# Seven products instead of eight in the up projection of a feed-forward

## Chip, cores, metric

One core of a Trainium2 chip. The metric is device time in microseconds (us), 3024.73 as the median of three runs.

## What is computed

One inference step of a one-layer encoder over 2048 prompt tokens and 128 sample tokens, 17 token tiles of 128, width 1024. After the attention and pooling mixers, the mix gives x1, and then:

```python
def conv_ffn(h, conv_hist, w_up, w_dw, b_dw, w_down):
    up = h @ w_up                       # 1024 -> 2 x 2816
    ext = concat([conv_hist, up])
    c = ext[:, 0:T] * w_dw[0] + ext[:, 1:T + 1] * w_dw[1] + ext[:, 2:T + 2] * w_dw[2] + b_dw
    a, b = split(c, 2)
    return (silu(a) * b) @ w_down, ext[:, -2:]
x1 = layer_norm(ALPHA * x + mix)
x2 = layer_norm(ALPHA * x1 + ffn + sigmoid(x1 @ w_pg) * (p @ w_pe))
```

Everything is float32. Each matrix operand is held as a high part (rounded, fp32r) and a low part (the rest), and a product is three matmuls: high x high, low x high, high x low.

## The kernel before, in words

Six phases run one after the other: project, heads and sample attention, attend, mix, ffn. The change touches the last two.

**mix** (line 1857) goes over the 17 token tiles. PE multiplies the mixed heads by w_o, ACT, DVE and POOL norm the result to x1, PE turns it (128 x 128 transposes, `turn`), ACT copies the turned tile to `x1_t` and splits it, PE multiplies it by w_pg (`gates`), ACT takes the sigmoid into `gate`, DVE forms ALPHA * x1 + gate * embedding there, and SP stores `x1_t` and `gate`. At its end the first weights and token pieces of the ffn are loaded and split (`AHEAD`).

**ffn** (line 2293) takes the tokens in three blocks of 6, 6 and 5 tiles (`BLOCKS`; the last holds the sample tokens). For a block it goes over 22 feature tiles f, two to a pair. An f has two halves, s = 0 (a, goes through silu) and 1 (b). The up projection of an f (`rows` and `part` of PE) is, for each half and each half of the block's tokens, 8 slices of the contraction x 3 matmuls: 2 x 2 x 24 = 96 matmuls, of 384 tokens (384 and 256 in the last block), into four PSUM banks. ACT copies a bank to `up` and begins the convolution (tap 2 and bias) into `cv`; DVE adds taps 1 and 0 (`convolve`); ACT takes silu; DVE multiplies the halves (`gate`) into `h`; ACT makes its high part and POOL its low part (`product_hi`, `product_lo`). After each pair PE multiplies by two tiles of w_down (`downs`: 12 matmuls of 512 columns a token tile), and DVE adds the results to `y` in SBUF (`add`). After the last pair of a block `y` is normed (`normalise`, `centre`).

Weights come in units of 128 x 1024 (512 KB), six to a pair, through three raw buffers: SP loads, ACT makes the high part (L2540), POOL the low part (L2467). The high and low parts of the six have places of their own (`EVEN`, `DOWN`, `ODD`). The order on each engine is written out by hand; each engine works through its own queue in order and waits on semaphores. PE's order in a loop step is `rows(2q + 2)`, `downs(q)`, `rows(2q + 3)`.

## Time and profile before

| | us |
|---|---|
| runs | 3021.55, 3024.73, 3024.91 |
| span of the profiled execution | 3021.1 |
| feed-forward, from about | 1442 |
| PE busy | 2938.2 |

An instruction's row has its line, engine, operation, tiles (buffer numbers left out), shape, and durations; `[x <- engine tile line]` is idle time before it and what ended it. Matmuls overlap in the rows, so the pace is read from starts. DVE is VectorE, ACT ScalarE, POOL GpSimd, SP the queue that issues DMAs, PEld the weight loads. The profile has one execution's own span; no other time of that execution is given.

### The profile page before, as it was taken

To read this page: it belongs to the slowest core of one execution; us is meant where nothing else is said; L and a number is where in the kernel's file an instruction comes from. 1 tells how busy PE (TensorE), PEld (TensorE's weight loads), DVE (VectorE), ACT (ScalarE), POOL (GpSimd) and SP (SyncE) were. 2 spreads that over 40 slices of the span, in tenths; PEclk is the share of its full clock that TensorE was granted. 3 is DMA by queue.
4 is the path that set the end of the run, shared out by engine and by line. 5 is a ranking of instruction groups with operands and counts; after the bars stand their busy time and mean duration, and the time that the engine had idled before them with its cause. 6 is when DMAs were issued, how large, how long until landed. Compare 5 with 4: busy or idle time off the path is not lost.

```text
span 3021.1 us, 43561 instructions
## 1 busy us (share of the span) xinstructions
PE 2938.2 (97%) x15389; PEld 2586.1 (86%) x15389; DVE 1618.7 (54%) x2178; ACT 1352.3 (45%) x2632; POOL 1393.3 (46%) x830
## 2 busy tenths in 40 slices
PE   8998999999999899999999999999999999999997
PEld 6877787777776688887999999999999998999996
DVE  5635776787776544443434444464444447454446
ACT  4342555877787222222433333443434344444443
POOL 5342554666766422222434343474343447443445
PEclk9997898999999999999999999999999999999998
DMA  4227452122213322222412121242121224221221
GB/s 137 87 66 144 137 174 58 43 55 52 47 43 130 120 89 89 89 89 96 175 53 72 56 69 56 96 155 70 56 69 56 69 70 150 102 72 67 80 72 61
DMA packets 161774, 262.10 MB, mean 87 GB/s; under 512 B 48352, under 2 KB 91072, under 8 KB 160288
## 3 DMA queue, kind: packets, MB, share of 16 engines
q1 hardware_dynamic: 161664, 260.69, 27.7%
q8 instruction: 62, 1.02, 0.1%
q14 instruction: 48, 0.39, 0.0%
HBM read 204.76 MB, written 55.88 MB: 86 GB/s over the span
## 4 chain that ended last, share of the span: by engine, by line
PE 51%; DVE 1%; POOL 0%; issue 0%; DVEq 0%; ACTq 0%
PE ff_u L84 12%; PE ff_u L86 12%; PE ff_u L85 11%; PE ff_d L84 6%; PE ff_d L85 6%; PE ff_d L86 6%; DVE ff_y L2682 0%; DVE ff_y L2731 0%; DVE ff_stats L2714 0%; POOL ff_y L2517 0%; POOL ff_rstd L2507 0%; DVEq L2297 0%; DVE ff_mv L2716 0%; DVE ff_neg_mean L2718 0%; POOL ff_offset L2509 0%
## 5 line engine op out<-in xcount | busy, mean ns | idle before, releaser
L2467 POOL TENSOR_TENSOR ff_w_lo<-ho_raw,ff_w_hi 128x1024 fp32r<-128x1024 f32 x99 | 242.9, 2467 | 491.1 <-ACT ff_w_hi L2540 491.1
L2467 POOL TENSOR_TENSOR mx_w_lo<-ho_raw,mx_w_hi 128x1024 fp32r<-128x1024 f32 x97 | 276.0, 2859 | 230.9 <-ACT mx_w_hi L2540 230.9
L2661 DVE SCALAR_TENSOR_TENSOR ff_cv_a<-ff_up_a,ff_taps,ff_cv_a 128x768 f32<-128x768 f32 (+1 forms) x132 | 154.7, 1172 | 346.9 <-ACT ff_cv_a L2589 338.9
L2682 DVE TENSOR_TENSOR ff_y<-ff_y,ff_d 128x512 f32<-128x512 f32 x374 | 239.6, 681 | 146.3 <-PE ff_d L86 146.2
L2661 DVE SCALAR_TENSOR_TENSOR ff_cv_b<-ff_up_b,ff_taps,ff_cv_b 128x768 f32<-128x768 f32 (+1 forms) x132 | 122.7, 929 | 305.4 <-ACT ff_cv_b L2589 296.8
L1564 POOL TENSOR_TENSOR at_p_lo<-at_p,at_p_hi 128x512 fp32r<-128x512 f32 (+2 forms) x160 | 187.6, 1173 | 163.9 <-ACT at_p_hi L1601 162.2
L84 PE MATMUL ff_u<-ho_hi,mx_w_hi 128*128 128x384 f32 (+1 forms) x690 | 224.9, 326 | 0.7 <-ACTq L2533 0.7
L86 PE MATMUL ff_u<-ho_lo,mx_w_hi 128*128 128x384 f32 (+1 forms) x690 | 225.0, 326 | 0.0
L85 PE MATMUL ff_u<-ho_hi,mx_w_lo 128*128 128x384 f32 (+1 forms) x690 | 224.8, 326 | 0.0
L1594 ACT ACTIVATE at_p<-at_s 128x512 f32<-128x512 f32 (+1 forms) x320 | 170.2, 532 | 111.1 <-PE at_s L1790 56.0
L1706 DVE TENSOR_TENSOR at_p_lo<-at_p,at_p_hi 128x512 fp32r<-128x512 f32 (+1 forms) x160 | 187.3, 1171 | 45.5 <-ACT at_p_hi L1601 44.6
L84 PE MATMUL ff_u<-ho_hi,ff_w_hi 128*128 128x384 f32 x630 | 205.1, 326 | 0.0
L86 PE MATMUL ff_u<-ho_lo,ff_w_hi 128*128 128x384 f32 x630 | 205.0, 325 | 0.0
L85 PE MATMUL ff_u<-ho_hi,ff_w_lo 128*128 128x384 f32 x630 | 205.0, 325 | 0.0
L1601 ACT ACTIVATE at_p_hi<-at_p 128x512 fp32r<-128x512 f32 (+1 forms) x320 | 179.0, 560 | 0.0
L2580 ACT ACTIVATE ff_up_b<-ff_u 128x384 f32<-128x384 f32 x110 | 54.2, 493 | 268.8 <-PE ff_u L86 268.8
L84 PE MATMUL ff_d<-ff_w_hi,ff_h_hi 128*128 128x512 f32 x408 | 159.1, 390 | 4.4 <-DVE ff_y L2682 4.4
L2473 POOL TENSOR_TENSOR ff_h_lo<-ff_h,ff_h_hi 128x768 fp32r<-128x768 f32 (+1 forms) x66 | 118.2, 1791 | 91.3 <-ACT ff_h_hi L2600 91.3
L2674 DVE TENSOR_TENSOR ff_h<-ff_cv_a,ff_cv_b 128x768 f32<-128x768 f32 (+1 forms) x66 | 158.0, 2393 | 3.6 <-ACT ff_cv_a L2611 0.4
L85 PE MATMUL ff_d<-ff_w_hi,ff_h_lo 128*128 128x512 f32 x408 | 159.1, 390 | 0.0
L86 PE MATMUL ff_d<-ff_w_lo,ff_h_hi 128*128 128x512 f32 x408 | 159.1, 390 | 0.0
L2540 ACT ACTIVATE ff_w_hi<-ho_raw 128x1024 fp32r<-128x1024 f32 x99 | 103.3, 1049 | 123.2 <-DMA ho_raw<-in_w_ffn_p 123.2
(496 smaller groups left out, 8863.7 us busy)
## 6 DMA issues: line engine op xcount, KB each, us to landing
ho_raw<-in_w_ffn_p SPq DMA_DIRECT2D x196, 512.0 KB, 3.6
ho_raw<-in_x SPq DMA_DIRECT2D x17, 512.0 KB, 4.3
mx_m_raw<-scratch_mix_t SPq DMA_DIRECT2D x17, 512.0 KB, 5.2
scratch_x_t<-mx_work SPq DMA_DIRECT2D x17, 512.0 KB, 3.2
scratch_y<-mx_work SPq DMA_DIRECT2D x17, 512.0 KB, 3.0
ff_y<-scratch_y SPq DMA_DIRECT2D x17, 512.0 KB, 6.2
out_y<-ff_y SPq DMA_DIRECT2D x17, 512.0 KB, 2.7
ho_raw<-in_x_t SPq DMA_DIRECT2D x32, 256.0 KB, 3.1
```

What stands on the lines that cost most here:

```text
L84: pe.matmul(out, lh, rh, start=first, stop=False, **kw)
L85: pe.matmul(out, ll, rh, start=False, stop=False, **kw)
L86: return pe.matmul(out, lh, rl, start=False, stop=last, **kw)
L1564: pool.tensor_tensor(p_lo[:, e % H_RING, 0:b - a], p[:, e % P_RING, 0:b - a], f32(p_hi[:, e % H_RING, 0:b - a]), ALU.subtract).then_inc(lo ...
L1594: act.activation(p[:, i % P_RING, 0:b - a], ps_s[i % S_BANKS][:, 0:b - a], ACT.Exp).then_inc(expd, 1)
L1601: act.activation(p_hi[:, i % H_RING, 0:b - a], p[:, i % P_RING, 0:b - a], ACT.Copy).then_inc(hid, 1)
L1706: dve.tensor_tensor(p_lo[:, e % H_RING, 0:b - a], p[:, e % P_RING, 0:b - a], f32(p_hi[:, e % H_RING, 0:b - a]), ALU.subtract).then_inc(lo_ ...
L2467: pool.tensor_tensor(w_lo[slot], w_raw[n % RAWS].rearrange("p (k c) -> p k c", c=P), f32(w_hi[slot]), ALU.subtract).then_inc(wlo, 1)
L2473: pool.tensor_tensor(h_lo[:, i + extra, 0:w], h[:, i, 0:w], f32(h_hi[:, i + extra, 0:w]), ALU.subtract)\
L2661: op = dve.scalar_tensor_tensor(cv[s][:, 0:pw], up[s][:, k:k + pw], tap, cv[s][:, 0:pw], ALU.mult, ALU.add)
L2674: dve.tensor_tensor(h[:, i, 0:w], cv[0][:, 0:w], cv[1][:, 0:w], ALU.mult).then_inc(mul, 1)
L2682: dve.tensor_tensor(y[:, t, H[i]], y[:, t, H[i]], ps_d[2 * (t % 2) + i][:, :], ALU.add)\
```

## The change

The up projection of an f is computed in Strassen's way (Winograd's form). The weights of an f are cut into four blocks, A11, A12 (half a; first and second half of the contraction) and A21, A22 (half b); the tokens of a block into B11, B21 (left 64 tokens of every tile; first and second half of the contraction) and B12, B22 (right 64). With S1 = A21 + A22, S2 = S1 - A11, S3 = A11 - A21, S4 = A12 - S2 and T1 = B12 - B11, T2 = B22 - T1, T3 = B22 - B12, T4 = B21 - T2, seven products remain: A11 B11, A12 B21, S2 T2, S1 T1, S3 T3, S4 B22, A22 T4, each 4 slices x 3 matmuls of half the block's tokens (384; 320 in the last block): 84 matmuls.

- Bank `ps_x` gathers A11 B11, then S2 T2, S3 T3, A22 T4 on top; after each ACT copies it to a quarter of `up` (`copy`). The other three products go to two more banks and DVE adds them to `up` (`join`, four an f). ACT begins the convolution from `up` (`begin`), the whole block's width.
- The token sums T1 to T4 are formed by POOL in the mix (`form`), from `x1_t`, whose quarters are now laid out for it, into `gate`, and stored; ACT's sigmoid waits for that store. Token operands are loaded as seven sets, 768 KB each, into their low tile and split there.
- The weight sums S1 to S4 are formed by POOL (`combine`), 512 wide. Each of the seven roles has one place for its high and low part (256 KB each), split for the next f once the role's product is done: high by ACT, low by DVE (`weights`; no role is left to POOL). POOL makes the low parts of w_down in four pieces of 256 KB that pass through one raw buffer, `d_raw`.
- DVE makes the low part of hidden (`hidden_low`), and gate and hidden use `cv` in place.
- Even f have w_down's products of the pair before between S3 and S4; at the start of a block they follow A11 and A12.

```diff
+            def form(t):
+                low_left, low_right, high_left, high_right = (x1_t[:, n * TILE_X:(n + 1) * TILE_X] for n in range(4))
+                t2, t1, t3, t4 = (gate[:, n * TILE_X:(n + 1) * TILE_X] for n in range(4))
+                pool.wait_ge(tcopy, at(t, 2, 1))
+                pool.wait_ge(st_y, (t + 1) * 16)
+                pool.tensor_tensor(t1, low_right, low_left, ALU.subtract).then_inc(formed, 1)
+                pool.tensor_tensor(t3, high_right, low_right, ALU.subtract).then_inc(formed, 1)
+                pool.wait_ge(formed, at(t, 4, 0))
+                pool.tensor_tensor(t2, high_right, t1, ALU.subtract).then_inc(formed, 1)
+                pool.wait_ge(formed, at(t, 4, 2))
+                pool.tensor_tensor(t4, high_left, t2, ALU.subtract).then_inc(formed, 1)
...
-                act.wait_ge(st_y, (t + 1) * 16)
+                act.wait_ge(st_x, (t + 2) * 48)
...
+            def even_loads(b, f, p, at_next, at_d):
+                nb, nf = following(b, f, 2)
+                load_down(b, p, at_d, 0)
+                if nb < 3:
+                    load_up(nb, nf, p + 1 if nb == b else 0, 0, at_next, (A11, A22, A12, S1))
+                load_down(b, p, at_d, 1)
+            def odd_loads(b, f, p, at_next, at_d):
+                nb, nf = following(b, f, 2)
+                turn = nb > b
+                load_down(b, p, at_d, 2)
+                for j in range(PRODUCTS):
+                    if turn and nb < 3:
+                        load_x(nb, j)
+                    if j in (0, 1, 3) and nb < 3:
+                        load_up(nb, nf, 0 if turn else p + 1, 1, at_next, {0: (A11, A22), 1: (A12,), 3: (S1,)}[j])
+                    if j == 1:
+                        load_down(b, p, at_d, 3)
...
+            def combine(b, f, pf, par, ops=range(4)):
+                pb, pf_ = following(b, f, -1)
+                a11, a12, s1, a22 = w_raw[:, A11, :], w_raw[:, A12, :], w_raw[:, S1, :], raw22(par)
+                s2, s3, s4 = w_raw[:, S2, :], w_raw[:, S3, :], w_raw[:, S4, :]
+                if 0 in ops:
+                    pool.wait_ge(combined, sum_n(pb, pf_, 3))
+                    pool.wait_ge(raw_in[A11], 16 * (b * FT + f + 1))
+                    pool.wait_ge(raw_in[S1], 16 * (b * FT + f + 1))
+                    weight_low(b, f, pb, pf_, S3)
+                    pool.wait_ge(*low_done(pb, pf_, S3))
+                    pool.tensor_tensor(s3, a11, s1, ALU.subtract).then_inc(combined, 1)
+                    pool.wait_ge(combined, sum_n(b, f, 0))
+                    pool.wait_ge(raw_in22[par], 16 * (b * PAIRS_F + pf + 1))
+                    pool.tensor_tensor(s1, s1, a22, ALU.add).then_inc(combined, 1)
+                    pool.wait_ge(combined, sum_n(b, f, 1))
+                    pool.tensor_tensor(s2, s1, a11, ALU.subtract).then_inc(combined, 1)
+                if 3 in ops:
+                    pool.wait_ge(combined, sum_n(b, f, 2))
+                    pool.wait_ge(raw_in[A12], 16 * (b * FT + f + 1))
+                    weight_low(b, f, pb, pf_, S4)
+                    pool.wait_ge(*low_done(pb, pf_, S4))
+                    pool.tensor_tensor(s4, a12, s2, ALU.subtract).then_inc(combined, 1)
...
+            def down_lows(b, p, parts):
+                for m in parts:
+                    pool.wait_ge(dhi, down_n(b, p, m))
+                    hi, lo = down_piece(b, p, m)
+                    pool.tensor_tensor(lo, d_raw[:, :], f32(hi), ALU.subtract).then_inc(dlo, 1)
...
                 with pool.Fori(0, LAST - 1) as q:
+                    combine(b, 2 * q + 3, q + 1, 1)
+                    combine(b, 2 * q + 4, q + 2, 0, (0, 1, 2))
+                    down_lows(b, q + 1, (0,))
+                    combine(b, 2 * q + 4, q + 2, 0, (3,))
+                    down_lows(b, q + 1, (1, 2, 3))
...
+            def weights(b, f, roles, pf=None, par=None):
+                for j in roles:
+                    raw = w_raw[:, j, :]
+                    if j == A22:
+                        act.wait_ge(raw_in22[par], 16 * (b * PAIRS_F + pf + 1))
+                        raw = raw22(par)
+                    elif j in (A11, A12):
+                        act.wait_ge(raw_in[j], 16 * (b * FT + f + 1))
+                    else:
+                        act.wait_ge(combined, sum_n(b, f, {S3: 0, S1: 1, S2: 2, S4: 3}[j]))
+                    nb, nf = following(b, f, -1)
+                    act.wait_ge(prod, per_f(nb, nf, PRODUCTS, j))
+                    act.activation(w[j][0], raw, ACT.Copy).then_inc(whi, 1)
...
+            def copy(b, f, par, k):
+                s, right, j = ((0, 0, A11), (0, 1, S2), (1, 1, S3), (1, 0, A22))[k]
+                pb, pf = following(b, f, -1)
+                act.wait_ge(conv, per_f(pb, pf, 4, 1 if s == 0 else 3))
+                act.wait_ge(prod, per_f(b, f, PRODUCTS, j))
+                for dst, src in halves_of(b, s, right, ps_x[par]):
+                    op = act.activation(dst, src, ACT.Copy)
...
+            def finish_up(b, f, p, i, par):
+                begin(b, f, p, i, 0)
+                carry_out(b, f, p, i, 0)
+                copy(b, f, par, 3)
+                begin(b, f, p, i, 1)
+                carry_out(b, f, p, i, 1)
...
+            def period(b, f, p, i, before, x_next=False, centring=None):
+                nb, nf = following(b, f, 1)
+                more = nb < 3
+                if before is not None:
+                    finish_up(*before)
+                carry_in(b, f, p, i, 0)
+                if before is not None:
+                    weights(b, f, (A22,), p, i)
+                    activate(*before[:4])
+                if i == 1:
+                    down_highs(b, p, (0, 1) if at_end(b, p) else (1,))
+                copy(b, f, i, 0)
+                if more:
+                    weights(nb, nf, (A11,))
+                carry_in(b, f, p, i, 1)
+                if before is not None:
+                    product_hi(*before[:4])
+                if more:
+                    weights(nb, nf, (A12,))
+                if i == 0 and isinstance(f, int) and f == 0:
+                    tokens(b, (T2, T1, T3, B22, T4) if b else (T3, B22, T4))
+                copy(b, f, i, 1)
+                if more:
+                    weights(nb, nf, (S2,))
+                if centring is not None:
+                    centre(b - 1, centring[0])
+                if i == 1:
+                    down_highs(b, p, (2,))
+                if more:
+                    weights(nb, nf, (S1,))
+                if centring is not None:
+                    centre(b - 1, centring[1])
+                if x_next:
+                    tokens(b + 1, (B11,))
+                copy(b, f, i, 2)
+                if more:
+                    weights(nb, nf, (S3,))
+                if x_next:
+                    tokens(b + 1, (B21,))
+                if not at_end(b, p) or i == 1:
+                    down_highs(b, p, (3,) if i == 1 else (0,))
+                if more:
+                    weights(nb, nf, (S4,))
...
+            def hidden_low(b, f, p, i):
+                hi, lo = hidden(b, p, i)
+                dve.wait_ge(hhi, b * FT + f + 1)
+                dve.tensor_tensor(lo, cv[0][:, 0:BLOCKS[b] * P], f32(hi), ALU.subtract).then_inc(hlo, 1)
...
+            def join(b, f, par, k):
+                s, right, bank, j, c = ((0, 0, ps_z, A12, 0), (0, 1, ps_y, S1, 1), (1, 1, ps_y, S3, 2),
+                                        (0, 1, ps_z, S4, 2))[k]
+                dve.wait_ge(prod, per_f(b, f, PRODUCTS, j))
+                dve.wait_ge(copied, per_f(b, f, 4, c))
+                if k == 3:
+                    dve.wait_ge(joined, per_f(b, f, 4, 1))
+                for dst, src in halves_of(b, s, right, bank):
+                    op = dve.tensor_tensor(dst, dst, src, ALU.add)
+                op.then_inc(joined, 1)
...
+            def period(b, f, par, before, adds=None, x_next=False, after_last=False, shifts=((), (), (), ())):
+                def shift_tiles(n):
+                    for t in shifts[n]:
+                        shift(b - 1, t)
+                nb, nf = following(b, f, 1)
+                more = nb < 3
+                if before is not None:
+                    convolve(*before, 0)
+                    convolve(*before, 1)
+                    gate(*before)
+                    weights(b, f, (A22,), par)
+                if more:
+                    weights(nb, nf, (A11,))
+                shift_tiles(0)
+                join(b, f, par, 0)
+                if before is not None:
+                    hidden_low(*before)
+                shift_tiles(1)
+                if more:
+                    weights(nb, nf, (A12,))
+                if after_last:
+                    for t in range(BLOCKS[b - 1]):
+                        add(b - 1, LAST, t)
+                        statistics(b - 1, t)
+                        if t == 1:
+                            tokens(b, (T2,))
+                        if t == 3:
+                            tokens(b, (B22,))
+                if b == 0 and isinstance(f, int) and f == 0:
+                    tokens(0, (B22,))
+                if more:
+                    weights(nb, nf, (S2,))
+                join(b, f, par, 1)
+                if more:
+                    weights(nb, nf, (S1,))
+                if x_next:
+                    tokens(b + 1, (B11,))
+                join(b, f, par, 2)
+                shift_tiles(2)
+                if more:
+                    weights(nb, nf, (S3,))
+                if x_next:
+                    tokens(b + 1, (B21,))
+                if adds is not None:
+                    if isinstance(adds[1], int) and adds[1] == 0:
+                        dve.wait_ge(y_in, 16 * (FIRST[b] + BLOCKS[b]))
+                    for t in range(BLOCKS[b]):
+                        add(*adds, t)
+                join(b, f, par, 3)
+                if more:
+                    weights(nb, nf, (S4,))
+                shift_tiles(3)
...
+            def multiply(b, f, par, roles, opening=False):
+                hw = HALVES[b]
+                pb, pf = following(b, f, -1)
+                qb, qf = following(b, f, -2)
+                for j in roles:
+                    if opening:
+                        if j in (T1, T3, T4):
+                            pe.wait_ge(xlo_pool, 3 * b + (T1, T3, T4).index(j) + 1)
+                        else:
+                            pe.wait_ge(xlo_dve, 4 * b + (B11, B21, T2, B22).index(j) + 1)
+                    pe.wait_ge(*low_done(b, f, j))
+                    if j == A11:
+                        pe.wait_ge(copied, per_f(qb, qf, 4, 3))
+                    elif j == A12:
+                        pe.wait_ge(joined, per_f(pb, pf, 4, 3))
+                    elif j == S2:
+                        pe.wait_ge(copied, per_f(b, f, 4, 0))
+                    elif j == S1:
+                        pe.wait_ge(joined, per_f(pb, pf, 4, 2))
+                    elif j == S3:
+                        pe.wait_ge(copied, per_f(b, f, 4, 1))
+                    elif j == S4:
+                        pe.wait_ge(joined, per_f(b, f, 4, 0))
+                    else:
+                        pe.wait_ge(copied, per_f(b, f, 4, 2))
...
+            before_downs, after_downs = (A11, A12, S2, S1, S3), (S4, A22)
             for b in range(3):
-                rows(b, 0, 0, ODD, opening=True)
-                rows(b, 1, 2, DOWN)
+                multiply(b, 0, 0, (A11, A12), opening=True)
+                if b > 0:
+                    downs(b - 1, LAST)
+                multiply(b, 0, 0, (S2, S1, S3, S4, A22), opening=True)
+                multiply(b, 1, 1, range(PRODUCTS))
                 with pe.Fori(0, LAST - 1) as q:
-                    n = 6 * q + 4
-                    rows(b, 2 * q + 2, n, EVEN)
-                    downs(b, q, n + 2)
-                    rows(b, 2 * q + 3, n + 4, ODD)
-                n = 6 * (LAST - 1) + 4
```

## Rows read from the trace of the kernel before

**Rows 1.** The page's first part: busy us (share of the span) and instructions, TensorE.
```profile
PE 2938.2 (97%) x15389; PEld 2586.1 (86%) x15389; DVE 1618.7 (54%) x2178; ACT 1352.3 (45%) x2632; POOL 1393.3 (46%) x830
```
**Rows 2.** Busy time by stretches: PE, PEld, DVE, ACT, POOL, granted clock, DMA share, GB/s.
```profile
1020.00:1040.00 20.00, 18.47 (x69) 15.08 (x70) 10.91 (x14) 4.80 (x8) 6.38 (x4) 0.83 0.15 44
...
1591.86:1641.53 49.67, 49.67 (x266) 46.82 (x265) 21.35 (x22) 18.60 (x35) 19.57 (x8) 1.00 0.19 63
...
2600.00:2641.80 41.80, 41.80 (x255) 39.44 (x254) 19.70 (x28) 18.25 (x46) 18.78 (x8) 1.00 0.22 76
1960.00:1980.00 20.00, 18.53 (x83) 15.04 (x82) 11.06 (x20) 8.46 (x11) 20.00 (x11) 1.00 0.41 132
```
**Rows 3.** Timeline of TensorE: start us, duration, line; 18 starts lie between each two.
```profile
1901.07 0.39 PE L84 MATMUL ff_d<-ff_w_hi,ff_h_hi 128*128 128x512 f32 x1
...
1905.15 0.39 PE L84 MATMUL ff_d<-mx_w_hi,ff_h_hi 128*128 128x512 f32 x1
...
1909.50 0.33 PE L84 MATMUL ff_u<-ff_x_hi,mx_w_hi 128*128 128x384 f32 x1
...
1912.62 0.33 PE L84 MATMUL ff_u<-ff_x_hi,mx_w_hi 128*128 128x384 f32 x1
```
**Rows 4.** Instructions by tile, VectorE: ns min/median/max, first and last start.
```profile
L2661 DVE SCALAR_TENSOR_TENSOR ff_cv_b<-ff_up_b,ff_taps,ff_cv_b x132: 744/1018/1022, 1461.8 to 2973.1; 128x768 f32<-128x768 f32 x88, 128x512 f32<-128x512 f32 x44
...
L2648 DVE TENSOR_TENSOR ff_x_lo<-ff_x_raw,ff_x_hi x3: 957/959/960, 1446.8 to 1449.0; 128x768 fp32r<-128x768 f32 x3
...
L2148 DVE TENSOR_TENSOR mx_t_lo<-mx_work,mx_t_hi x34: 684/693/695, 1020.7 to 1424.1; 128x512 fp32r<-128x512 f32 x34
...
L2682 DVE TENSOR_TENSOR ff_y<-ff_y,ff_d x374: 672/680/690, 1495.6 to 3004.6; 128x512 f32<-128x512 f32 x187
...
L2674 DVE TENSOR_TENSOR ff_h<-ff_cv_a,ff_cv_b x66: 821/2849/3100, 1464.3 to 2975.2; 128x768 f32<-128x768 f32 x44, 128x640 f32<-128x640 f32 x22
```
**Rows 5.** The same for GpSimd, an operation 512 wide.
```profile
L360 POOL TENSOR_TENSOR ho_lo<-ho_raw,ho_hi x24: 1253/1288/1721, 45.9 to 258.7; 128x512 fp32r<-128x512 f32 x24
```
**Rows 6.** The same for ScalarE.
```profile
L2077 ACT ACTIVATE mx_t_hi<-mx_t x34: 591/604/618, 1019.6 to 1423.4; 128x512 fp32r<-128x512 f32 x34
...
L2580 ACT ACTIVATE ff_up_a<-ff_u x110: 470/494/494, 1457.5 to 2965.2; 128x384 f32<-128x384 f32 x110
...
L2562 ACT ACTIVATE ff_y<-ff_y,ff_offset,ff_rstd x17: 1228/1244/1252, 1986.3 to 3009.0; 128x1024 f32<-128x1024 f32 x17
...
L2611 ACT ACTIVATE ff_cv_a<-ff_cv_a x66: 723/832/847, 1463.4 to 2972.4; 128x768 f32<-128x768 f32 x44, 128x640 f32<-128x640 f32 x22
```
**Rows 7.** Timeline of VectorE and of GpSimd, twice: start us, duration.
```profile
1942.59 3.10 DVE L2674 TENSOR_TENSOR ff_h<-ff_cv_a,ff_cv_b 128x768 f32<-128x768 f32 x1
...
1942.47 5.49 POOL L2467 TENSOR_TENSOR ff_w_lo<-ho_raw,ff_w_hi 128x1024 fp32r<-128x1024 f32 x2 [3.79 <-ACT ff_w_hi L2540]
...
2096.37 1.27 DVE L2682 TENSOR_TENSOR ff_y<-ff_y,ff_d 128x512 f32<-128x512 f32 x2
...
2093.13 5.58 POOL L2467 TENSOR_TENSOR mx_w_lo<-ho_raw,mx_w_hi 128x1024 fp32r<-128x1024 f32 x2 [9.23 <-ACT mx_w_hi L2540]
```
**Rows 8.** DMA issues: count, KB each, median us from issue to landing.
```profile
ho_raw<-in_x_t SPq DMA_DIRECT2D x32, 256.0 KB, 3.1
...
ho_raw<-in_w_in_p SPq DMA_DIRECT2D x18, 256.0 KB, 3.9
```
**Rows 9.** Timeline of VectorE at a block's end, two tiles' additions.
```profile
1979.85 1.27 DVE L2682 TENSOR_TENSOR ff_y<-ff_y,ff_d 128x512 f32<-128x512 f32 x2
...
1982.85 1.27 DVE L2682 TENSOR_TENSOR ff_y<-ff_y,ff_d 128x512 f32<-128x512 f32 x2
```
**Rows 10.** Timeline of ScalarE and GpSimd in the mix, one token tile.
```profile
1070.45 0.60 ACT L2076 ACTIVATE mx_work<-mx_t 128x512 f32<-128x512 f32 x1
...
1086.25 1.09 ACT L2087 ACTIVATE mx_work<-mx_g 128x512 f32<-128x512 f32 x2 [9.16 <-PE mx_g L86]
...
1076.01 0.55 POOL L2017 TENSOR_TENSOR mx_rstd<-mx_var_eps,mx_power 128x1 f32<-128x1 f32 x1 [18.96 <-DVE mx_var_eps L2133]
```

918 lines of the change are left out of this document (518 added, 400 removed).

## The prediction

> **What bounds the kernel now.** I read the page first: TensorE (PE) is busy 97% of the span [rows 1]. Then one steady pair of feature tiles (two f) in a block of six token tiles and in the last block of five, by the view of busy time by stretches: 49.67 and 41.8 us, PE busy all of it, VectorE (DVE) 21.4 and 19.7 us, GpSimd (POOL) 19.6 and 18.8, ScalarE (ACT) 18.6 and 18.3 [rows 2]. So the feed-forward is a plain stream of matmuls. The timeline gives their pace: 18 starts of 384 columns in 3.12 us, 0.1733 each, and 18 of 512 columns in 4.08 us, 0.2267 each [rows 3]. The pair adds up: 192 x 0.1733 + 72 x 0.2267 = 49.6. In the last block, 41.8 less 60 x 0.2267 less 96 x 0.1733 leaves 0.120 for a matmul of 256 columns; 320 columns lie halfway, 0.1467.
>
> **What goes.** An up projection of one f is 84 matmuls instead of 96, each of half the block's tokens. Twelve of 384 columns are 2.08 us less an f, or 4.16 a pair (PE floor 45.5 against 49.67); in the last block 84 x 0.1467 = 12.3 against 14.1, a floor of 38.2 a pair. Over 22 and 11 pairs: 92 + 39 = 131 us. That is the most the change can give. The Trainium skill (TensorE: Matmul & The Clock Gate, Back-to-back issue gap) has columns / 2.4 plus 2.5 ns for lone streams, 162 ns for 384 columns; by it the gain would be nearer 122, by the rows 131. The rows' pace decides.
>
> **What comes, by engine, an f of a six-tile block.** Prices from [rows 4] (DVE), [rows 5] (POOL), [rows 6] (ACT).
> - DVE: 4 convolution passes at 1.02, the gate 0.96 (the 768-wide subtraction that met no POOL work), 7 low halves of weights at 0.69 (POOL's before), the low half of hidden 0.96 (POOL's), 4 joins of 384 columns, priced between nothing shown and 0.68, I take 0.55; six additions to y at 0.68. Together 17.1 us; PE's floor is 22.7.
> - POOL: 4 combinations of weights and 2 low halves of w_down, 512 wide, at 1.29: 7.7 us.
> - ACT: 7 + 2 high halves at 0.60, 4 copies 0.49, two 768-wide begins (between the 0.83 of silu, as wide, and the 1.24 of the 1024-wide centring with scale and bias; I take 1.0), silu and the high half of hidden 0.83 each: 11.0 us and four short carries. It has room in sum, but it is in order.
>
> **The port.** DVE and POOL stand in each other's way. A gate of 0.96 us took 3.10 where a POOL subtraction had just begun, and the POOL operation behind it was stretched in turn; additions out of PSUM kept to 1.27 for two with POOL at work [rows 7]. So a two-input SBUF operation of DVE waits for the POOL operation in flight. Thirteen of DVE's 23 operations an f are of that kind now, where 5 were. The Trainium skill (SBUF — State Buffer, Who interferes with whom) says this speaks against the change: the shared ports are an exclusive lock for the whole instruction. Rows 7 agree; if the two shared bandwidth instead, the sum would keep most of the gain. DVE plus POOL is 24.8 us an f, over PE's 22.7. In odd periods (no w_down products, no additions) it is worse: DVE 13.0, POOL up to 7 x 1.29 = 9.0, PE only 7 x 2.08 = 14.6. In even periods PE has 30.9 us and DVE about 21, so it catches up.
>
> **The chain.** Product S2 adds to the bank of A11, and waits for ACT's copy of it (copied 0). In ACT's order that copy stands behind carry_in (waits for the convolution of a of the f before), the A22 high, silu and, in odd periods, a w_down high. After the convolution of a that is 0.1 + 0.5 + 0.8 + 0.45 = 1.9 us, 2.4 in odd periods. Time 0 is the end of an even period's A22.
> - Odd period: convolution of a starts at 0, meets POOL's S4 combination (begun when DVE's S4 low ended), ends 3.1; the copy ends 5.6; S2 was due at 4.16. PE loses 1.5.
> - w_down passes through one raw buffer now: piece 1 is split by ACT at about 5, by POOL until 6.6, the next load (256 KB, 3.1 to 3.9 us [rows 8]) lands at 9.8, is split until 11.6, the last lands at 14.8 and its high is done at 15.3. ACT's S4 high stands behind it: 15.8, where S4's product was over at 14.1. Begin of a ends at 16.9.
> - Now POOL has its last w_down low and four combinations ready, all next to the convolutions. Without conflict the convolution of a ends at 18.3 to 19, the copy at 20.3; if DVE and POOL alternate, at 21.4 and 23.4. PE's own pace has S2 at 18.7. I take 22.9, since the gate paid so at the median: 2.85 us over 66 of them, 0.82 where a 640-wide one met nothing [rows 4].
> - The hidden low (gate, two lows, a join, then it) is at most 0.4 late for the w_down products, which follow S1 and S3.
> After S2 starts, PE needs 3 x 2.08 + 16.3 + 2 x 2.08 = 26.7. Pair: 22.9 + 26.7 + 0.4 = 50.0, against 49.67: the saving is eaten, +7 us over 22 pairs. In the last block the chain hardly shortens (the sample rows have operations of their own, +0.4) while PE's part does: 23.3 + 5.3 + 13.6 + 3.5 + 0.4 = 46.1 against 41.8, +47 us over 11.
>
> **Ends of blocks.** Before, each cost PE 1.5 us or so [rows 2]. Now w_down's last products come after A11 and A12 only, 4.2 us into the period, and need a hidden low that is there at 8 to 14; operand sets are 1536 wide, and ACT, in order, waits for their 768 KB loads, each longer than the 3.9 us of 256 KB; DVE adds six tiles, their statistics (3.0 us a tile against PE's 2.7, as before [rows 9]) and two 1.65 us splits, and shifts and scales now run within the next periods. I take 15 each, between 5 and 25: +30. First opening: T3 and T4 are loaded and split late, +5 (0 to 10).
> **The mix.** POOL forms four sums a token tile, 5.2 us, and SP issues two stores more. POOL was idle 19 us before each rstd there [rows 10]; the sum before it may push rstd by a microsecond, and turning the tile is later still. Sigmoid now waits for the store of the sums, some 9 us after the tile's last copy (5.2 and a store); it came 15.8 us after that copy before, behind PE's gate matmuls (same rows). Nothing; if that cover were gone, 17 tiles at 1 us. SP's two more issues a tile, and the history, taps and norm loads that only change places, have nobody waiting behind them.
>
> **Sum.** 7 + 47 + 30 + 5 = 89 on the profiled execution's span of 3021.1: 3110. The median, 3024.7, is 3.6 above the span, so 3114. A difference under 0.2% is about what a measurement can't tell from none.
>
> **Rivals.**
> - **The chain is shorter (faster).** If S2 of an even period starts before 20.2 us after the odd period's start, the kernel gains; break-even: 22 x (s - 22.57) + 11 x (s - 18.6) + 35 = 0, from the pairs above with s in place of 22.9. For it: ACT and DVE have gaps where POOL's work could fall, and several POOL operations wait for loads. Without any conflict and with cheap block ends (5 each) it is s = 20.3 and 3009; at s = 19.3 it is 2976. Chance 0.15, 2965 to 3018.
> - **PE stays the bound.** S2 at 18.7: 131 less 15 for block ends, 2908. Against it: it needs DVE at 13.0 us plus conflicts inside 14.6. Chance 0.12, up to 2965.
> - **No change.** Gains of the six-tile blocks and losses of the last cancel: 0.12.
> - **Full alternation and the clock.** s = 23.5 and block ends at 25: 3024.7 + 20 + 54 + 50 + 10 = 3159. In a stretch in which PE was busy 18.5 of 20 us the granted clock was 0.83 [rows 2], part of it at 1.2 GHz instead of 2.4; PE would now pause 1 to 4 us in every period. If the clock fell like that, it would pass 3200. Chance 0.13 for over 3160.
> - **Forecast**: slower, 3031 to 3160, chance 0.48.
> Range for 8 in 10: 2950 to 3180; the likeliest case's own is 3060 to 3160. Faster 0.27, same 0.12, slower 0.61.
>
> **What would show it.** In the profile after: 84 matmuls an f at 0.173 apart; a pair of about 50 us and of 46 in the last block; PE idle before the S2 product, released by ACT's copy, 1.5 us in odd and 4 in even periods; DVE busy above 75% in the feed-forward, with its two-input operations lengthened; ACT's S4 high waiting behind a w_down load. I am wrong if a pair takes under 48 us, if PE waits for something else (a low half, hidden), if POOL's combinations fall in even periods beside the additions, or if the mix has grown.

## The result, and the profile after

The changed kernel takes 3301.64 us (median of four runs, 3297.84 to 3303.71), the kernel before 3023.14 on the same chip: a ratio of 1.0924, 95% interval 1.0909 to 1.0940. Slower was forecast, but at 3114, and 3302 lies far outside the range of 2950 to 3180. The profiled execution has a span of 3300.3 us, 279.2 more than before.

The page's first part, busy time (share of the span) and instructions, against [rows 1]:

```profile
span 3300.3 us, 47350 instructions
PE 2918.2 (88%) x14597; PEld 2540.4 (77%) x14597; DVE 2228.4 (68%) x3062; ACT 1478.7 (45%) x2981; POOL 1417.7 (43%) x1023
```

In the steady pairs TensorE was busy all the time before [rows 2]; now it is not. Its waits say for what (what waited, for whom, us in total, times, longest):

```profile
PE ff_u L84 <- ACT ff_up_a L2800: 235.1, 65, 10.3
PE ff_d L84 <- issue: 20.9, 2, 10.6
PE ff_d L84 <- DVE ho_raw L3003: 17.1, 4, 9.4
PE ff_uz L84 <- DVE ff_up_a L2967: 12.3, 4, 4.8
PE ff_u L84 <- ACT ff_up_b L2800: 11.6, 7, 7.0
```

The first row is product S2 waiting for ACT's copy 0, once an f: the wait that the prediction named. Busy time by stretches (PE, PEld, DVE, ACT, POOL, granted clock, DMA share, GB/s), a steady stretch of the first block, a pair of the last and the opening, against the 49.67 us and 41.80 us fully busy of [rows 2]:

```profile
1600.00:1800.00 200.00, 181.82 (x901) 168.67 (x902) 146.80 (x175) 81.04 (x158) 70.12 (x46) 0.95 0.19 62
1450.00:1500.00 50.00, 27.61 (x132) 26.70 (x132) 27.10 (x23) 18.88 (x32) 23.32 (x12) 0.78 0.56 178
2993.00:3044.00 51.00, 41.00 (x229) 38.10 (x228) 36.80 (x61) 22.49 (x63) 16.64 (x13) 0.90 0.19 62
```

**Where the time went.** The start of silu of an f marks the same point in every kernel, so each kernel's feed-forward is cut at silu of f = 4 and f = 18 of every block: seven steady pairs a block, and between them the opening (from 1442.5 us), two block ends (four pairs each) and the tail. In microseconds:

```
                 median  opening  pair b0  pair b1  pair last  end 1  end 2  tail
before             3023    100.8    49.67    49.67      41.78  200.3  185.1 104.6
after              3302    156.3    53.02    52.98      51.13  254.0  242.6 105.1
e1_fill            3252    146.6    51.44    51.58      49.21  250.3  240.9 104.5
e2_port            3275    151.1    52.67    52.65      48.55  252.6  243.3 106.2
e3_copy_first      3256    151.3    51.46    51.38      49.64  251.5  241.2 100.8
e13_port_even      3223    152.5    50.21    49.72      47.11  249.7  242.1 105.3
e7_two_raw         3262    139.1    52.14    51.84      51.23  249.6  244.3  98.5
e6_dh3_port        3218    145.8    49.76    50.35      48.74  247.6  237.4 101.2
e4_dh3_late        3173    147.5    48.76    48.89      45.36  245.5  233.8 101.0
e8_dh3_copy        3164    150.0    48.44    48.58      45.17  243.1  232.6  98.5
e9_candidate       3143    132.8    48.36    48.51      45.19  242.1  230.9  98.2
e10_s4_first       3162    129.4    49.31    49.49      46.12  241.0  231.6 101.0
e11_end_piece      3145    130.4    48.34    48.58      45.21  245.1  231.5  98.8
e12_no_tokens      3287    153.8    52.83    52.99      51.23  245.8  238.2 105.5
```

Of the 279 us, 47 are the first two blocks' steady pairs, 65 the last block's, 111 the two ends, 55 the opening. The mix took nothing: the first matmul of the feed-forward stood at 1442.14 and stands at 1442.55.

All experiments but e13_port_even ran once, beside one run of the kernel before, which lay between 3021.7 and 3024.1 in all of them. The four runs of e13_port_even lie between 3213.8 and 3228.8. So a difference of some 10 us between two kernels that ran once says nothing by itself; the steady pairs of the table, 7 to a block, and the traces say more.

**One steady pair.** Timelines (start us, duration, engine, line, the idle time before and who ended it) of the second half of an odd period that began at 1806.89, ACT first:

```profile
1822.12 0.63 ACT L2784 ACTIVATE ho_hi<-ff_d_raw 128x512 fp32r<-128x512 f32 x1 [2.24 <-DMA ff_d_raw<-in_w_ffn_p]
1822.66 0.62 ACT L2775 ACTIVATE mx_w_hi<-ff_w_raw 128x512 fp32r<-128x512 f32 x1
1823.18 1.02 ACT L2835 ACTIVATE ff_cv_a<-ff_up_a,ff_taps 128x768 f32<-128x768 f32 x1
...
1828.81 0.20 ACT L2809 ACTIVATE ff_up_a<-ff_carry 128x2 f32 x1 [2.79 <-DVE ff_cv_a L2979]
1828.96 0.63 ACT L2775 ACTIVATE ho_hi<-ff_w_raw 128x512 fp32r<-128x512 f32 x1
1829.50 0.83 ACT L2852 ACTIVATE ff_cv_a<-ff_cv_a 128x768 f32<-128x768 f32 x1
1830.23 0.47 ACT L2800 ACTIVATE ff_up_a<-ff_u 128x384 f32<-128x384 f32 x1
```

DVE (S4's low half, then two passes of each convolution) and POOL (w_down's last low half, then the combinations):

```profile
1823.31 1.37 DVE L2949 TENSOR_TENSOR mx_w_lo<-ff_w_raw,mx_w_hi 128x512 fp32r<-128x512 f32 x1 [1.80 <-ACT mx_w_hi L2775]
1824.60 4.00 DVE L2979 SCALAR_TENSOR_TENSOR ff_cv_a<-ff_up_a,ff_taps,ff_cv_a 128x768 f32<-128x768 f32 x2
1828.52 3.97 DVE L2979 SCALAR_TENSOR_TENSOR ff_cv_b<-ff_up_b,ff_taps,ff_cv_b 128x768 f32<-128x768 f32 x2
...
1822.83 1.29 POOL L2688 TENSOR_TENSOR ho_lo<-ff_d_raw,ho_hi 128x512 fp32r<-128x512 f32 x1 [4.01 <-ACT ho_hi L2784]
1824.09 1.75 POOL L2671 TENSOR_TENSOR ff_w_raw<-ff_w_raw 128x512 f32<-128x512 f32 x1
1826.01 1.78 POOL L2674 TENSOR_TENSOR ff_w_raw<-ff_w_raw 128x512 f32<-128x512 f32 x1 [0.17 <-POOL ff_w_raw L2671]
```

ACT waits 2.24 us for w_down's last piece with S4's high half queued behind it; DVE then starts its convolutions together with POOL's combinations, and each pass takes 2.0 us instead of 1.02. Copy 0 ends at 1830.70 and S2 starts 23.9 us after the odd period's start. TensorE, the two S2 products of this pair and the matmuls behind the second:

```profile
1812.33 0.44 PE L84 MATMUL ff_u<-mx_odd,mx_w_hi 128*128 128x384 f32 x1 [1.11 <-ACT ff_up_a L2800]
...
1830.76 0.69 PE L84 MATMUL ff_u<-mx_odd,mx_w_hi 128*128 128x384 f32 x1 [3.60 <-ACT ff_up_a L2800]
1831.25 0.52 PE L85 MATMUL ff_u<-mx_odd,mx_w_lo 128*128 128x384 f32 x1
1831.57 0.52 PE L86 MATMUL ff_u<-mx_odd,mx_w_hi 128*128 128x384 f32 x1
...
1836.94 0.34 PE L85 MATMUL ff_uy<-mx_odd,mx_w_lo 128*128 128x384 f32 x1
1837.12 0.34 PE L86 MATMUL ff_uy<-mx_odd,mx_w_hi 128*128 128x384 f32 x1
```

Behind the pause of 3.60 us, 17 matmuls start 0.32 us apart, not 0.173, and the granted clock of the stretch is 0.95, not 1.00: TensorE runs at the lower of its two clocks (1.2 GHz). Behind that of 1.11 us it keeps the higher (2.4).

### The profile page after: what moved, and what is told of

It is laid out like the page before. It is cut to its first block and busy times, and to the rows that moved or that the text cites. A ratio compares the mean times of both kernels' runs of the same rounds, so it can differ in the third digit from the quotient of the medians.

```text
span 3300.3 us, 47350 instructions
## 1 busy us (share of the span) xinstructions
PE 2918.2 (88%) x14597; PEld 2540.4 (77%) x14597; DVE 2228.4 (68%) x3062; ACT 1478.7 (45%) x2981; POOL 1417.7 (43%) x1023
## 3 DMA queue, kind: packets, MB, share of 16 engines
q1 hardware_dynamic: 203056, 274.08, 27.1%
## 5 line engine op out<-in xcount | busy, mean ns | idle before, releaser
L2949 DVE TENSOR_TENSOR mx_w_lo<-ff_w_raw,mx_w_hi 128x512 fp32r<-128x512 f32 x390 | 323.4, 840 | 98.2 <-ACT mx_w_hi L2775 94.3
L84 PE MATMUL ff_u<-mx_odd,mx_w_hi 128*128 128x384 f32 (+1 forms) x264 | 118.2, 448 | 234.0 <-ACT ff_up_a L2800 234.0
L3003 DVE TENSOR_TENSOR ho_raw<-ho_raw,ff_d 128x512 f32<-128x512 f32 x264 | 169.3, 684 | 183.9 <-PE ff_d L86 162.7
L2775 ACT ACTIVATE mx_w_hi<-ff_w_raw 128x512 fp32r<-128x512 f32 x390 | 242.9, 623 | 85.3 <-PE ff_uy L86 44.5
L2671 POOL TENSOR_TENSOR ff_w_raw<-ff_w_raw 128x512 f32<-128x512 f32 x65 | 98.7, 1519 | 369.5 <-DMA ff_w_raw<-in_w_ffn_p 368.2
L84 PE MATMUL ff_d<-mx_odd,ff_h_hi 128*128 128x512 f32 x364 | 144.8, 398 | 38.1 <-issue 20.9
L1679 DVE TENSOR_REDUCE at_neg_max<-mx_m 128x1 f32<-128x512 f32 (+2 forms) x214 | 128.3, 604 | 46.9 <-PE mx_m L1755 26.0
L86 PE MATMUL ff_d<-mx_odd,ff_h_hi 128*128 128x512 f32 x364 | 143.9, 395 | 0.0
L85 PE MATMUL ff_d<-mx_odd,ff_h_lo 128*128 128x512 f32 x364 | 143.9, 395 | 0.0
L1810 PE MATMUL at_o<-at_p_hi,at_v_one 128*66 128x512 f32 (+1 forms) x320 | 119.4, 373 | 3.4 <-DVE at_p_lo L1708 2.2
L2682 POOL TENSOR_TENSOR ff_w_raw<-ff_w_raw 128x512 f32<-128x512 f32 x65 | 99.5, 1531 | 46.5 <-DVE mx_w_lo L2949 41.7
L3003 DVE TENSOR_TENSOR ff_y<-ff_y,ff_d 128x512 f32<-128x512 f32 x110 | 70.6, 684 | 71.7 <-PE ff_d L86 71.7
```

Of the source, the lines that this page charges most:

```text
L84: pe.matmul(out, lh, rh, start=first, stop=False, **kw)
L85: pe.matmul(out, ll, rh, start=False, stop=False, **kw)
L86: return pe.matmul(out, lh, rl, start=False, stop=last, **kw)
L1679: dve.tensor_reduce(neg_max[:, tile % 4, c:c + 1], ps_m[n % M_BANKS][:, 0:peak_width(n)], AX.X, ALU.max, negate=True).then_inc(reduced, 1)
L2775: act.activation(w[j][0], raw, ACT.Copy).then_inc(whi, 1)
L2949: dve.tensor_tensor(w[j][1], raw, f32(w[j][0]), ALU.subtract).then_inc(wlo_dve, 1)
```

## The experiments

Three causes lie on one path to S2: **ring** (w_down through one raw buffer, its high halves in ACT's list), **port** (convolutions beside combinations) and ACT's **order** ahead of copy 0. The **clock** is a fourth, behind the pause. The diffs are against the changed kernel, shortened.

**e1_fill: the clock.**

```diff
-                    multiply(b, 2 * q + 2, 0, before_downs)
+                    multiply(b, 2 * q + 2, 0, before_downs[0:2])
+                    fill(b, q, 14 if b < 2 else 28)   # matmuls into ps_d[0], whose result nobody reads
+                    multiply(b, 2 * q + 2, 0, before_downs[2:])
```

> Nothing of the computation is left out; in the even period of every pair of the loop, between the products A12 and S2, TensorE runs extra products whose result nobody reads (14 of 512 columns in the first two blocks, 3.2 us by the pace of 0.227; 28 in the last block, 6.3 us), into a bank of down sums that is free there. They fill the pause ahead of S2. Theory CLOCK (the pause costs twice: once itself, once by the slow matmuls behind it, which take 0.32 us instead of 0.17 for about 20 starts): S2 begins at the same time as in the changed kernel, the matmuls behind it keep 0.17, a pair of the first block takes about 50.5 us instead of 53.5, the last block about 48.5 instead of 51.1, the kernel about 3301 - 9 x (3 + 3 + 2.6) = 3220. Rival (the chain through VectorE sets every pair, so that a faster TensorE only waits longer at the next product): pair within 0.5 us of 53.5, kernel within 15 of 3301.

3252, 49 us less, for extra work. The granted clock of 1600 to 1800 us is 1.00 instead of 0.95, and S2 starts no earlier (24.0 us after the odd period's start in the mean of the first block's pairs, 23.8 in the changed kernel): only the slow matmuls are gone. So the clock is a true cost, but of 1.6, 1.4 and 1.9 us a pair instead of the 3, 3 and 2.6 expected. The trace of the changed kernel shows most of why. The pauses ahead of S2 in one stretch, 3.42, 3.53, 3.60 and 3.50 us, were followed by 17, 10, 17 and 10 slow starts, 0.147 us each: 2.0 us in the mean, not 3.

**e2_port: the port, with a mistake in it.**

```diff
-                    combine(b, 2 * q + 3, q + 1, 1)
+                    combine(b, 2 * q + 3, q + 1, 1, late=(0,))      # late: waits for mul of the f before
-                    combine(b, 2 * q + 4, q + 2, 0, (3,))
+                    combine(b, 2 * q + 4, q + 2, 0, (3,), late=(3,))
```

> Nothing is left out; only GpSimd's order changes: in the loop the weight combinations for an odd period (the first and the fourth of them, and so all four) wait until the gate product of the period before has been written, so they no longer run beside the convolutions of the even period's opening. Theory PORT (the convolutions at 2.0 us instead of 1.1 each, from sharing with GpSimd): they take 4.3 us together instead of 8, S2 of the even period begins about 20.5 us after the odd period's start instead of 23.8, the pause ahead of it falls under 1 us and with it the clock's fall; pair of the first block 47 to 49 us instead of 53.5, kernel 3120 to 3190. Rival WAITS (what holds S2 is ScalarE's wait for the last piece of w_down and its own order; the convolutions stretch only into slack): S2 moves by under 1 us, kernel within 20 of 3301. Second rival: the combinations come 6 us later and their splits are late for the odd period: a new pause ahead of its products, kernel not faster.

3275, only 27 less, although the two passes of the even period's half a took 2.17 us instead of 4.00. S2 still started 23.7 us after the odd period's start. GpSimd's rows show what took the gain back (the odd period began at 1802.03):

```profile
1807.49 1.61 POOL L2686 TENSOR_TENSOR ff_w_raw<-ff_w_raw 128x512 f32<-128x512 f32 x1 [7.45 <-DVE ff_cv_a L2994]
1809.07 1.74 POOL L2692 TENSOR_TENSOR mx_odd<-ff_d_raw,mx_odd 128x512 fp32r<-128x512 f32 x1
```

The second wait that I had put in held up the fourth combination, and behind it in GpSimd's list stands the low half of w_down's second piece: it ended 8.8 us after the odd period's start, where it had ended 7.1 after. The rest of the ring (w_down's load, high half, low half and next load, all through one buffer) came 1.7 us later, and 1.8 is what the convolution of half a had gained. Read without that, the run says that the port hardly matters. The kernel with the first wait alone was run last:

**e13_port_even: the port alone** (the first changed line of e2_port, without the second; four runs).

> Nothing is left out. e2_port held back two things: the combinations for the odd periods (meant) and the fourth combination for the even ones, behind which w_down's second piece is queued on GpSimd, so that its ring began 1.7 us later and took back the 1.8 us that the convolution of half a had gained. Here only the first stays, one wait ahead of the first combination for an odd period. Theory CHAIN of both (port and ring add on one path): the even S2 comes 23.9 - 1.8 = 22.0 us after the odd period's start, its pause is 1.8 us, at which the clock does not fall (it fell behind pauses of 3.1 us and over, not behind 2.1), so the first two blocks' pair goes from 53.0 to 49.5 to 50.5 us; in the last block, where the four instructions of half a took 6.0 us instead of some 2.5, from 51.1 to 46 to 48; kernel 3301 - 22 x 3 - 9 x 4 = about 3200. Rival (the port matters only with the ring gone, as e2_port read at face value): within 15 of 3275.

3222.7 us against 3023.4, ratio 1.0657 (1.0633 to 1.0682): 79 less than the changed kernel. S2 starts 22.2 us after the odd period's start (22.0 expected), pairs take 50.2, 49.7 and 47.1. The first theory holds. One part of it fell, that the clock stays up behind pauses of some 2 us: in this trace the pauses of 2.38 (at 1764.81) and 1.90 us (at 1815.43) were followed by 9 and 10 slow starts, that of 2.33 (at 1915.67) and those of 1.73, 1.63 and 1.11 by none. The trace of the changed kernel could have told: in its last block a pause of 2.12 us (at 2838.96) was followed by 12 slow starts, another of 2.12 (at 2940.88) by none.

In the last block the port costs more. Instructions on the convolution of half a, from 2850 to 3050 us, ns min/median/max, first the changed kernel, then this one. Half of the 16 belong to the even period's opening, where GpSimd combines; the other half meet no combination in either kernel:

```profile
L2979 DVE SCALAR_TENSOR_TENSOR ff_cv_a<-ff_up_a,ff_taps,ff_cv_a x16: 752/1352/1782, 2851.4 to 3039.6; 128x512 f32<-128x512 f32 x16
L2982 DVE SCALAR_TENSOR_TENSOR ff_cv_a<-ff_up_a,ff_taps,ff_cv_a x16: 339/845/1354, 2853.1 to 3040.3; 128x128 f32<-128x128 f32 x16
```
```profile
L2981 DVE SCALAR_TENSOR_TENSOR ff_cv_a<-ff_up_a,ff_taps,ff_cv_a x16: 739/752/1107, 2877.1 to 3035.8; 128x512 f32<-128x512 f32 x16
L2984 DVE SCALAR_TENSOR_TENSOR ff_cv_a<-ff_up_a,ff_taps,ff_cv_a x16: 339/342/348, 2878.1 to 3036.5; 128x128 f32<-128x128 f32 x16
```

The timeline of the changed kernel has the four of one opening one by one, beside four combinations:

```profile
3004.31 1.75 DVE L2979 SCALAR_TENSOR_TENSOR ff_cv_a<-ff_up_a,ff_taps,ff_cv_a 128x512 f32<-128x512 f32 x1
3005.99 1.34 DVE L2982 SCALAR_TENSOR_TENSOR ff_cv_a<-ff_up_a,ff_taps,ff_cv_a 128x128 f32<-128x128 f32 x1
3007.47 1.60 DVE L2979 SCALAR_TENSOR_TENSOR ff_cv_a<-ff_up_a,ff_taps,ff_cv_a 128x512 f32<-128x512 f32 x1
3008.99 1.34 DVE L2982 SCALAR_TENSOR_TENSOR ff_cv_a<-ff_up_a,ff_taps,ff_cv_a 128x128 f32<-128x128 f32 x1
...
3003.80 1.72 POOL L2671 TENSOR_TENSOR ff_w_raw<-ff_w_raw 128x512 f32<-128x512 f32 x1
3005.69 1.50 POOL L2674 TENSOR_TENSOR ff_w_raw<-ff_w_raw 128x512 f32<-128x512 f32 x1 [0.17 <-POOL ff_w_raw L2671]
3007.26 1.26 POOL L2676 TENSOR_TENSOR ff_w_raw<-ff_w_raw 128x512 f32<-128x512 f32 x1
3008.68 1.51 POOL L2682 TENSOR_TENSOR ff_w_raw<-ff_w_raw 128x512 f32<-128x512 f32 x1 [0.16 <-POOL ff_w_raw L2676]
```

An instruction of 128 columns, 0.34 us by itself, takes 1.0 us longer here; one of 512, 0.75 by itself, 0.85 to 1.0; one of 768 in a six-tile block, 1.02 by itself, 1.0. So the price goes by the instruction, not by its width. The four take 6.0 us here, the two of a six-tile block 4.0. The Trainium skill (SBUF — State Buffer, Who interferes with whom) calls the port pair that the two engines share an exclusive lock, held for the whole instruction. These rows agree: the 1.0 us is the same for 128 columns as for 768, and engines that only shared bandwidth would be expected to lengthen the wider one more.

**e3_copy_first: ACT's order.**

```diff
                 carry_in(b, f, p, i, 0)
+                copy(b, f, i, 0)
                 if before is not None:
                     weights(b, f, (A22,), p, i)
                     activate(*before[:4])
                 if i == 1:
                     down_highs(b, p, (0, 1) if at_end(b, p) else (1,))
-                copy(b, f, i, 0)
```

> Nothing is left out; only ScalarE's order changes: copy 0 (the join's first quarter, which frees the bank that S2 writes) comes right behind the carry columns, ahead of A22's high half, the silu and, in odd periods, w_down's high halves. Theory CHAIN (S2 waits for the convolution of half a, then ScalarE's list, then the copy): S2 of the even period comes 0.63 + 0.83 = 1.4 us earlier, of the odd one 1.9; the even pause is then about 2.2 us, the odd one gone; pair 53.5 - 1.4 - 1.1 = 51.0, and 48 if the clock no longer falls behind the shorter pause; kernel 3235 (3155 with the clock). Rival (silu, gate, and the low halves behind them come later by the copy's 0.47 and are next on the path): within 10 of 3301.

3256, 45 less. The odd pause is gone in the six-tile blocks, but the even one is 3.54 to 4.12 us there, as before, for ACT now waits 3.15 us for the last piece of w_down instead of 2.24: it comes to it earlier, and the ring does not.

```profile
1811.53 0.63 ACT L2784 ACTIVATE ho_hi<-ff_d_raw 128x512 fp32r<-128x512 f32 x1 [3.15 <-DMA ff_d_raw<-in_w_ffn_p]
```

The even S2 starts 22.7 us after the odd period's start instead of 23.8, and those 1.1 us are the odd period's pause.

**e4_dh3_late: the ring.** 

```diff
                 # end of the odd period
-                if not at_end(b, p) or i == 1:
-                    down_highs(b, p, (3,) if i == 1 else (0,))
+                if not at_end(b, p) and i == 0:
+                    down_highs(b, p, (0,))
                 ...
                 copy(b, f, i, 0)      # even period
+                if i == 0 and before is not None:
+                    down_highs(before[0], before[2], (3,))
```

> Nothing is left out; ScalarE's high half of w_down's last piece, which stands at the end of the odd period ahead of S4's high half and waited 2.24 us there for its transfer, moves into the next period behind copy 0 (GpSimd's low half of it and the weight combinations queued behind that follow it there). Theory RAW BUFFER (the single buffer of w_down delays the piece, the piece delays S4's high half, that S4's low half on VectorE and the convolutions behind it): S4's low half starts 1.8 us earlier and S2 of the even period 1.8 earlier; and since GpSimd's combinations move behind the convolutions, the port's share goes too (3.3 more): the pause vanishes, pair 47 to 48 us, kernel 3110 to 3160. By the waits alone, if the port doesn't count: pair about 50, kernel 3210. Rival: the piece's low half or the combinations come too late, and TensorE waits at the down products or at S4: a pause there of the size of the one taken away, kernel within 20 of 3301.

3173, 129 less, the largest single step; but it takes two things away. The piece's low half now comes behind copy 0 too, and the combinations queued behind it in GpSimd's list no longer run beside the convolutions: the two passes of half a took 2.18 us. S2 starts 20.5 us after the odd period's start, and pairs take 48.8, 48.9 and 45.4 us.

**e6_dh3_port: the ring gone, the port back.**

```diff
                     combine(b, 2 * q + 3, q + 1, 1)
+                    down_lows(b, q, (3,))
                     combine(b, 2 * q + 4, q + 2, 0, (0, 1, 2))
                     ...
-                    down_lows(b, q + 1, (1, 2, 3))
+                    down_lows(b, q + 1, (1, 2))
```

> Nothing is left out. As e4_dh3_late on ScalarE (w_down's last piece is split behind copy 0 of the next period), but GpSimd's list puts the four weight combinations ahead of that piece's low half again, so that they can run beside the even period's convolutions as in the changed kernel. With the changed kernel (ring and port: 3302), e2_port (ring, no port: 3275) and e4_dh3_late (neither: 3173) it closes a square of four. Theory RING (w_down's one raw buffer paces the even S2 through transfer, high half, low half, transfer; the port's share only fills ring time): within 25 of 3173, pair 48.7 to 49.7. Rival PORT (with the ring gone, 3.6 us of slower convolutions come back onto the path): S2's pause in the even period 3 us or more, the clock falls behind it, pair 51.5 to 53, kernel 3240 to 3290.

3218, between what the two theories gave. With e13_port_even it closes a square:

```
                        with the ring's wait   without it
combinations beside            3302               3218
combinations behind            3223               3173
```

The port is worth 79 us with the ring and 45 without; the ring 83 with the port and 50 without. They lie on one path, and each hides some 34 us of the other (two of the four ran once, so this may be off by some 10). Of the port's 45 us, 24 are the last block's seven pairs (48.7 against 45.4).

**e7_two_raw: is it the buffer?** `d_raw` gets two halves and two semaphores, and piece m waits for the low half of piece m - 2. To make room the kernel leaves out the last norm's shift: its tile and its load are gone, and the gain is added instead.

> The changed kernel with two raw buffers for w_down instead of one, each with its own semaphore, every order kept; to make room the last layer norm's gain tile stands in for its shift tile too, so one load of the constants is gone and the output's last addition adds the gain. Theory RING: ScalarE finds the last piece landed (no 2.24 us wait), S4's low half and the convolutions start about 2 us earlier; the convolutions are still slowed by the combinations, so about the same as e6_dh3_port: pair 50 to 52, kernel 3200 to 3250 with the port on the path; 3170 to 3190 if the port is only filling. Rival (ScalarE's own list, not the transfer, sets the time): pair within 0.5 of 53, kernel within 20 of 3301.

3262, 40 less, of which 17 in the opening (one load fewer may have a part in them) and 14 in the steady pairs, 0.9 and 1.1 us shorter in the first two blocks and no shorter in the last. ACT still waited, 1.70 us instead of 2.24. SyncE's queue says why:

```profile
1797.58 0.33 SPq L2551 DMA_DIRECT2D ff_w_raw<-in_w_ffn_p  x1
1798.25 0.33 SPq L2561 DMA_DIRECT2D ff_d_raw<-in_w_ffn_p  x1
```

The last piece's buffer came free at 1794.1, when the low half of the second piece ended. Its load was issued at 1798.25, for it stands behind A12's reload in SyncE's queue. A second buffer is worth little while one in-order queue feeds both; moving the work that waits, with the port left as it was (e6), was worth 83 us, twice as much.

**e8_dh3_copy, e9_candidate.** e8 is e3 and e4 together. e9 adds three lines at the edges (each moved from its old place):

```diff
+            sp.dma_start(taps[:, :, :, :], g["taps"]).then_inc(const_in, 16)   # first of all loads
             load_up(0, 1, 0, 1, 1, (A11, S1, A22, A12))
+                odd_loads(b, 1, 0, 3, (-1, 12))       # ahead of the loads of y, gains and history
+                    if after_last:
+                        hidden_low(*before)           # directly behind the gate
```

> Nothing is left out: e4_dh3_late and e3_copy_first together (copy 0 right behind the carry columns). In e4 the loop of the first block still pauses 1.1 us ahead of the odd period's S2, the last block's 2.1 and 1.4 a pair, and single pauses of 9 us stand ahead of S2 near the blocks' starts, each with copy 0 queued behind a high half of w_down that waits for its transfer. Theory CHAIN: those shrink: first two blocks' pair 48.7 to 47.7, last block's 45.2 to about 42.5, and 4 to 8 us at each of four places: kernel 3173 - 18 - 24 - 24 = about 3107. Rival (the copy is followed by silu, gate and low halves which come later by its 0.4 and stall the down products): 3160 to 3180.

> Nothing is left out: e8_dh3_copy, and at the edges: the convolution taps are loaded first of the feed-forward stage's transfers (ScalarE waited 10.95 us for them ahead of the first copy 0), the loads of y, gains and history come behind w_down's third and fourth pieces (one of them landed 10.3 us late behind six y tiles), and at the block ends the hidden low half follows the gate directly (the last down products waited 9.15 us for it behind two weight low halves that ran slowly beside GpSimd). Expected against e8: opening -10 for the taps and -6 for the piece, block ends -3.4 each: -20 to -25, of the 33 + 77 us that the edges took more than forecast. Rival (the edges wait next for something else, the first combinations or token splits): -10 or less.

e8: 3164, where 3107 was expected. The odd pause is gone, but the down products now wait 1.38 us for the hidden low half, as the rival had it. e9: 3143, 21 less than e8, within its expectation: 17 in the opening, 3 at the two ends. Its steady pairs of six tiles, 48.4 and 48.5 us, are 1.2 shorter than those of the kernel before (49.67): there the change gives part of what it was made for, and that is lost in the last block, at the ends and in the opening. These are the rows of the changed kernel that e9 answers to, ACT in the opening:

```profile
1456.57 0.20 ACT L2809 ACTIVATE ff_up_a<-ff_carry 128x2 f32<-128x2 f32 x1 [11.00 <-DMA ff_taps<-in_taps]
...
1500.19 0.63 ACT L2784 ACTIVATE ff_d_own<-ff_d_raw 128x512 fp32r<-128x512 f32 x1 [10.69 <-DMA ff_d_raw<-in_w_ffn_p]
```

**e10_s4_first, e11_end_piece: two ways on from e9, both closed.** e10 has S4 in `before_downs`, its join and low half ahead of the additions, and w_down's first high half behind the begins; e11 keeps the last piece of a block in its old place.

> Nothing is left out: e9_candidate with S4 moved ahead of the down products in every even period, VectorE's last join and S4's low half ahead of the additions of down sums, and the high half of w_down's first piece from the even period's end to the next period behind the bias copies. In e9 the first two blocks' pair takes 48.5 us, 1.4 of it a pause of the down products for the hidden low half, 0.8 inside them for the additions. Theory: S4's 2.1 us cover the first, and the convolutions' start no longer waits for S4 behind the down products, so the last block's 1.85 us pause ahead of the odd S2 shrinks too: pair 48.5 to 47.0, last block 45.2 to 43.5, kernel 3143 - 27 - 15 = 3101. Rival (the odd S2 is one product nearer to the down products, 2.1 us, and the last additions still come ahead of the convolutions: a pause there takes the gain): within 15 of 3143 or slower.

> Nothing is left out: e9_candidate, with w_down's last piece of a block split at the end of the odd period again, as in the changed kernel, for the down products of a block's last pair come right behind the next block's first two products and in e9 waited 5.8 us for its low half. Expected: that pause gone at two places and the wait for the transfer ahead of S4's high half back (2.2 at two places, off TensorE's path by what slack there is): -5 to -12 against e9. Rival (the down products wait for the hidden low half at the same time, so that they start no earlier): within 3 of 3143.

e10: 3162, 19 more; the additions stand behind S4's join and low half, the down products wait 1.37 us for them in place of the hidden half, and a new pause of 1.47 us stands ahead of the odd period's S3. e11: 3145, no difference that one run can show, and its first end is 3 us longer, not shorter: the rival.

**e12_no_tokens: what the operand sets cost at the ends.**

> The changed kernel, in which the second and third block leave out loading and splitting their own token operands (7 loads, 7 high halves, 7 low halves a block) and go on with those of the first block, so y of these blocks is not the reference's; all else stays. The changed kernel takes 137 and 134.5 us from the last steady pair of a block to the first of the next, 36 and 41 more than the kernel before, where I had forecast 15. Theory SETS (seven 1536-wide operand sets in ScalarE's, VectorE's and GpSimd's lists make the ends): 20 to 30 us less at each of the two ends, kernel 3240 to 3265. Rival EDGE ORDER (the ends pay for w_down's ring, the hidden low half behind slowed low halves, and the additions with statistics; the splits run beside these): 0 to 10 less at each, kernel 3280 to 3302.

It leaves out the second and third block's own operands and goes on with the first block's. 3287: 8 and 4 us less at the two ends, as the rival had it: most of what the ends cost is not the loading and splitting of the sets.

No version here beats the kernel before: the best is e9_candidate, 3143 against 3022 beside it.

## Why the prediction was wrong in size and right in direction

**The steady pair of six-tile blocks: mechanism right, two terms off.** Forecast: S2 22.9 us after the odd period's start, then 27.1, in sum 50.0. Measured, in the mean: 23.8 and 29.2. The steps of the chain came close: the last piece's high half forecast at 14.8, found at 15.2; the begin's end at 16.9, found at 17.3; begins 1.0 (1.02), joins 0.55 (0.55). The first error is the value taken between 20.3 (no conflict) and 23.5 (full alternation): I took 22.9 by the median of the gates, and the trace has full alternation, two passes in 4.0 us, behind a begin that ended 0.4 late. The second and larger is the clock, for which the sum had no term: slow starts of 2.0 us a pair, of which filling the pause (e1) gave 1.5 back. [Rows 2] had shown a granted clock of 0.83 in one stretch with gaps and 1.00 in another with as many; I put it into a rival of 0.13 without a price. 3.3 us over 22 pairs is 73 us, where 7 were forecast.

**The last block.** Forecast 46.1, measured 51.1. S2 comes 26.2 us after the odd start instead of 23.3. The step that failed is "the chain hardly shortens (the sample rows have operations of their own, +0.4)": they were priced by their own time, 0.34, and each took 1.0 us more beside a combination. The other 2.1 are mostly the clock: filling gave 1.9 back. Over the nine pairs that the change lengthened: 84 us for 47.

**Block ends.** Measured without their steady pairs: 254.0 - 4 x 53.0 = 42 against 1.6 before, and 34 against 2; so 73 us for 30, over the bound of 25 each. The step that failed is the 15 each, put together from the down products, the sets and the additions at the turn itself: at the first end TensorE paused seven times for 1.5 us or more, 43 us in all, and five of the seven, 31 us, stand in the two periods behind. Rows of that end: the hidden low half and the down products behind it; two shifts in DVE's list; the loads of y, the addition behind them and the down products behind that:

```profile
2050.61 0.94 DVE L2995 TENSOR_TENSOR ff_h_lo<-ff_cv_a,ff_h_hi 128x768 fp32r<-128x768 f32 x1
2051.66 0.76 PE L84 MATMUL ff_d<-mx_odd,ff_h_hi 128*128 128x512 f32 x1 [10.31 <-issue]
...
2117.66 4.50 DVE L3019 TENSOR_TENSOR ho_raw<-ho_raw,ff_ln_b 128x1024 f32<-128x1024 f32 x2
...
2137.85 1.76 SPq L2571 DMA_DIRECT2D ho_raw<-scratch_y  x4
2148.70 0.69 DVE L3003 TENSOR_TENSOR ho_raw<-ho_raw,ff_d 128x512 f32<-128x512 f32 x1 [11.73 <-DMA ff_y<-scratch_y]
2150.04 0.79 PE L84 MATMUL ff_d<-mx_odd,ff_h_hi 128*128 128x512 f32 x1 [9.44 <-DVE ho_raw L3003]
```

- The down products waited 10.3 us for the hidden low half, forecast as "there at 8 to 14" where 4.2 was due.
- S2 paused 9.3 us at 2096.01; ACT had waited 4.2 us for a piece of w_down ahead of copy 0.
- A12 paused 4.2 us at 2116.35 and S2 6.8 us at 2127.07; DVE's list has two shifts of the block before ahead of the join (2108.20, 5.96 us for both) and two ahead of the convolution (2117.66).
- The down products of the new block's first pair paused 9.4 us, and 6.2 at the second end (2769.24), for additions that waited for the new tiles of y. Nothing in the prediction names these loads. SyncE issues them when the old tiles are stored, and the stores wait for the shifts, which now run within the next periods: issued at 2137.85, the last one landed at 2148.68. In the kernel before they were issued at 2013.03, 39 us behind the start of the block's last down products (1973.77); here it is 86 (2051.66). No experiment moved them, and in e9_candidate this pause is the longest that is left in the feed-forward, 12.2 us at 2085.61.

e12 shows the operand sets to be 12 us of the 73; the shares of the other parts are read from pauses, and no run took them apart.

**The opening.** 49 us besides its pairs, where 5 were forecast, the largest error in proportion. That "the history, taps and norm loads that only change places, have nobody waiting behind them" is the step that failed: ACT waited 11.0 us for the taps, which now stood behind the stage's first seven loads, and 10.7 for a w_down piece behind the norm's constants, the history and six tiles of y. e9 won 17 back by order alone. The other 32 were not taken apart; in e9's trace TensorE still pauses there, 7.3 us at 1459.28 and 5.5 at 1481.85.

**Right:** that the whole floor saving of 131 us would be eaten, and by the wait of S2 for ACT's copy; the port; S4's high half behind a w_down load; the mix at nothing. The forecast's error adds up: 66 (six-tile pairs) + 37 (last block) + 43 (ends) + 44 (opening) = 190 us, which is 3300 less 3110.

**The rivals.** Full alternation with the falling clock ("it would pass 3200") is what happened and had 0.13. The chain as I had written it out spoke for it: it had the convolutions and four combinations ready at the same moment, and 66 gates that met GpSimd by chance don't tell what two full lists do then.

## What to carry to other kernels

When a change moves work from a full engine to idle ones, sum the chain from product to product and not the busy times: here no engine but TensorE was busy for more than 68% of the span, and the kernel lost 9%. Two-input work out of SBUF on VectorE and GpSimd that becomes ready at the same time should be priced at full alternation, and by the number of instructions (1.0 us for each here). Where a wait is taken off one path, look at what is queued behind it on every in-order list, SyncE's and GpSimd's too: two of these edits (e2, e3) gave part of their gain back that way, and a second buffer behind an unchanged queue gave half of what moving one instruction did (40 us against 83). And where work is put off past a turn between blocks, follow what waits for it there: the shifts put off here held back the stores, the stores the loads of y, and these the additions.

## What the runs showed of the hardware that was not expected

- Pauses of equal length are not followed by the same clock. Between 1500 and 3150 us in the traces of the changed kernel and of e13_port_even: behind none of 54 pauses of 0.8 to 1.8 us came slow matmuls; behind 13 of 30 of 1.8 to 2.4 us came 9 to 12, behind the other 17 none; behind each of 59 longer ones came 5 to 21. Behind the 3.5 us pauses of the first block it was 10 or 17, at 0.32 us a start instead of 0.173: 1.5 to 2.5 us besides the pause. Filling the pauses with matmuls whose result nobody reads won 49 us.
- A 128-column operation of VectorE took 1.34 us beside GpSimd instead of 0.34, and the combinations beside 768-column passes 1.75 to 1.86 instead of 1.29: both engines lose.
